# A hybrid layer step on one core: another order of loads and mixer work, and six constant matmuls ahead of the norm

## The reference

```python
xn = rms_norm(h, norm_mix); q, k, v, u = split(xn @ w_in, [512, 640, 768])
# attention: 8 heads of 64, 2 kv heads, window 128, ALiBi, sinks; samples attend a cache of 128
attn = window_attend(q, k, v, sinks)
# S5: 32 groups of 16 inputs and 64 complex states
lam_bar = exp(lam * step); b_bar = (lam_bar - 1) / lam * b
x[t] = lam_bar * x[t-1] + b_bar @ u[t];  y = gelu(real(c @ x) + d * u)
ssm = y * sigmoid(y @ w_glu + b_glu)
h = h + concat(rms_norm(attn), rms_norm(ssm)) @ w_out
h = h + moe(rms_norm(h))          # 32 experts, 4 per token, 1024 -> 2048 -> 1024, clipped SwiGLU
h = h + sigmoid(rms_norm(h) @ w_ple_gate) * (p @ w_ple_proj)
return rms_norm(h), new k and v windows, new states
```

## Time and profile before

| what | us |
|---|---|
| median of 3 runs (lowest, highest) | 1359.23 (1357.03, 1359.85) |
| the profiled execution | 1358.6 |
| its span | 1356.8 |
| TensorE busy in the span | 1239.3 (91%) |
| VectorE, ScalarE busy | 327.5 (24%), 200.7 (15%) |
| mean granted clock | 0.946 |
| first matmul of the output projection | 190.30 |

### The profile page before, as it was taken

One profiled execution on the slowest core, in us unless ns is written; L12 is line 12 of the kernel. 1 busy time (PEld: TensorE's weight loads), 2 busy tenths in 40 slices (PEclk: granted clock), 3 DMA queues, 4 the chain that ended last, 5 costly groups with the idle time before them and its releaser, 6 DMA issues.

```text
span 1356.8 us, 15894 instructions
## 1 busy us (share of the span) xinstructions
PE 1239.3 (91%) x6158; PEld 608.7 (45%) x6158; DVE 327.5 (24%) x574; ACT 200.7 (15%) x385; POOL 19.8 (1%) x51
## 2 busy tenths in 40 slices
PE   2689778989999999999999999999999999999875
PEld 2577556524344343434344443434344443434354
DVE  4862323202112211111212211111112211120132
ACT  3412521201010101101010101011011101110022
POOL 1000000000000000000000000000000000000000
PEclk9769679989999999999999999999999999998888
DMA  8004523297999999999999999999999999998500
GB/s 261 1 32 169 224 75 124 77 397 323 422 399 422 405 418 417 406 424 406 422 394 422 407 408 418 384 424 403 423 410 422 389 421 398 409 381 369 192 2 32
DMA packets 73262, 438.47 MB, mean 323 GB/s; under 512 B 13617, under 2 KB 16817, under 8 KB 22497
## 3 DMA queue, kind: packets, MB, share of 16 engines
q1 hardware_dynamic: 67264, 436.98, 79.1%
q10 hardware_dynamic: 5968, 1.08, 0.5%
HBM read 436.67 MB, written 2.41 MB: 324 GB/s over the span
## 4 chain that ended last, share of the span: by engine, by line
PE 87%; DVE 5%; ACT 4%; issue 2%; ACTq 2%; DVEq 0%
PE ps L895 38%; PE ps L912 18%; PE ps L881 10%; PE ps L851 5%; PE ps L784 2%; PE ps L1024 2%; PE ps L903 2%; PE ps L854 1%; PE ps L585 1%; ACTq L1052 1%; PE ps L967 1%; PE ps L921 1%; PE ps L720 1%; PE ps L567 1%; PE ps L661 1%
## 5 line engine op out<-in xcount | busy, mean ns | idle before, releaser
L895 PE MATMUL ps<-ring_up,region 128*64 128x512 f32 x2112 | 463.5, 596 | 2.6 <-issue 1.4
L895 PEld LDWEIGHTS ps<-ring_up,region 128*64 128x64 f32 x2112 | 164.2, 138 | 283.9 <-issue 282.1
L912 PE MATMUL ps<-ring_dn,region 128*64 128x512 f32 x1056 | 247.3, 623 | 12.4 <-issue 11.0
L1801 DVE TENSOR_SCALAR region<-ps 128x512 f32<-128x512 f32 x33 | 22.8, 692 | 716.4 <-PE ps L895 716.4
L912 PEld LDWEIGHTS ps<-ring_dn,region 128*64 128x64 f32 x1056 | 82.9, 143 | 163.5 <-issue 161.6
L881 PE MATMUL ps<-region,n_tok 128*128 128x128 f32 (+1 forms) x768 | 136.1, 307 | 0.0
L881 PEld LDWEIGHTS ps<-region,n_tok 128*128 128x128 f32 (+1 forms) x768 | 104.2, 187 | 41.2 <-issue 12.2
L1284 ACT ACTIVATE region<-region 128x512 f32<-128x512 f32 x33 | 20.8, 629 | 501.3 <-DVE region L1801 501.3
L1296 ACT ACTIVATE region<-ps 64x512 f32<-64x512 f32 x66 | 39.1, 592 | 270.3 <-PE ps L912 269.9
L851 PE MATMUL ps<-region 128*128 128x512 f32 (+1 forms) x136 | 65.9, 606 | 2.6 <-issue 1.3
L895 PE MATMUL ps<-region 128*64 128x512 f32 x264 | 62.7, 592 | 0.0
(11 more groups left out here) (361 smaller groups left out, 758.1 us busy)
## 6 DMA issues: line engine op xcount, KB each, us to landing
ring_up<-in_w_up_dram SPq DMA_DIRECT2D x264, 1024.0 KB, 11.9
ring_dn<-in_w_down_dram SPq DMA_DIRECT2D x132, 1024.0 KB, 7.7
ring_dn<-in_w_out_dram SPq DMA_DIRECT2D x1, 4096.0 KB, 21.2
ring_up<-in_w_ple_gate_dram SPq DMA_DIRECT2D x4, 1024.0 KB, 7.4
ring_up<-in_w_in_dram SPq DMA_DIRECT2D x2, 1536.0 KB, 16.8
ring_up<-in_w_in_dram SPq DMA_DIRECT2D x2, 1024.0 KB, 9.8
x_tok<-in_x_prompt_dram SPq DMA_DIRECT2D x2, 512.0 KB
ring_up<-in_w_glu_dram SPq DMA_DIRECT2D x1, 1024.0 KB, 5.6
```

The costliest lines, as they stand in the source:

```text
L895: m = mm(ps[64 * (q % 2):64 * (q % 2) + 64, q // 2, :], xe[:, k, slots] if k < UP else one_hot, w, start=(k == 0), stop=(k == UP))
L912: m = mm(ps[64 * half:64 * half + 64, O_B, :], act_t[:, f % 4, 64 * (f // 4):64 * (f // 4) + 64], ring_dn[:, f, 512 * half:512 * half + 51 ...
L1801: V.tensor_scalar(g_lim, bank(0), LIMIT, None, ALU.min).then_inc(Z["g_rdy"], 1)
```

## The change

In the diff "..." marks what is left out. The six small loads of b, c and the sample states leave ScalarE's queue and stand in SyncE's between the u columns and the q, k, v columns of w_in. The constants get a semaphore of their own, and TensorE multiplies six times the identity by the first 512 columns of the constants into bank 6, which nobody reads, when they are there. On all engines the mixer is reordered: the turning of c and of the states goes between u projections, the projections of k, v and q go between the pieces of the drive, the second half of the read-out matrix goes between the two scans, and in the second part the gated unit goes ahead of the samples' attention and the probabilities of block 1. The turnings of c and of the states, written in line before, become the functions `turn_outputs` and `turn_sample_states`. On ScalarE all copies of u come in one run ahead of the sines and of the copies of turned drive blocks. Banks change with it (`project_one`, `ssm_sums`).

```diff
--- before.py
+++ after.py
@@ -311,7 +312,7 @@
         @block.sync
         def _(sp):
             x_p, x_s = A["x_prompt"][0], A["x_sample"].rearrange("b l d -> (b l) d")
-            sp.dma_start(kst[:], A["shape_constants"]).then_inc(ld_x, 16)
@@ -323,9 +324,18 @@
-                    sp.dma_start(w_in[:, k:k + 4, cols], w[:, k:k + 4, cols]).then_inc(arrived, 16)
+            of_s5, of_heads = slice(D_IN - D_SSM, D_IN), slice(0, D_IN - D_SSM)
+            for k in range(0, KD, 4):
+                sp.dma_start(w_in[:, k:k + 4, of_s5], w[:, k:k + 4, of_s5]).then_inc(ld_wu, 16)
+            for r, name in enumerate(("ssm_b_re", "ssm_b_im")):
+                sp.dma_start(b_raw[:, r], A[name][0].rearrange("(k g) p h -> (g p) k h", g=2)).then_inc(ld_b, 16)
+            for r, name in enumerate(("ssm_c_re", "ssm_c_im")):
+                sp.dma_start(c_raw[:, r], A[name][0].rearrange("(k g) h p -> (g h) k p", k=4)).then_inc(ld_c, 16)
+            for r, name in enumerate(("state_ssm_re", "state_ssm_im")):
+                sp.dma_start(rows[:, (10 + r) * P:(11 + r) * P],
+                              A[name][0].rearrange("b (k g) p -> (b k) (g p)", g=2)).then_inc(ld_x0, 16)
+            for k in range(0, KD, 4):
+                sp.dma_start(w_in[:, k:k + 4, of_heads], w[:, k:k + 4, of_heads]).then_inc(ld_win, 16)
             sp.dma_start(sink_b, A["sinks"][0].partition_broadcast(P)).then_inc(ld_sink, 16)
             for b_ in range(NB):
                 sp.dma_start(sink_s[HEADS * b_:HEADS * (b_ + 1), :], A["sinks"][0].unsqueeze(1)).then_inc(ld_sink, 16)
...
@@ -452,7 +462,11 @@
         def _(pe):
             mm, tr = nc.tensor.matmul, nc.tensor.transpose
 
-            pe.wait_ge(ld_x, 64)
+            pe.wait_ge(ld_k, 16)
+            for _ in range(6):
+                mm(bank(6), ident, kst[:, 0:512], start=True, stop=True)
+
+            pe.wait_ge(ld_x, 48)
             pe.wait_ge(ld_vec, 16 * 7)
             tr(bank(7, V_N), rows[0:V_N, 0:P], ident[0:V_N, 0:V_N]).then_inc(Z["vec_ps"], 1)
 
...
@@ -588,11 +606,13 @@
 
             def project_one(n_):
 
-                slot, b = (4, 5, 0, 1, 2, 3)[n_], 6 + n_ % 2
+                slot, b = (4, 5, 0, 1, 2, 3)[n_], (6, 7, 2, 3, 2, 3)[n_]
                 if n_ == 0:
                     pe.wait_ge(ld_win, 32)
-                    pe.wait_ge(Z["x_states"], 1)
-                if n_ >= 2:
+                    pe.wait_ge(Z["turned_sb"], 2)
+                elif n_ == 2:
+                    pe.wait_ge(Z["us_sb"], 1)
+                elif n_ >= 4:
                     pe.wait_ge(Z["q_sb"], n_ - 1)
                 if slot >= 4:
                     m = project(slot, b, lambda k: w_in[:, k, D_ATTN + (slot - 4) * P:D_ATTN + (slot - 3) * P])
...
                     pe.wait_ge(Z["ssm_sq"], c + 1)
-                    m = mm(bank(5, T), ones, sq[:, c % 2], start=(c == 0), stop=(c == KM - 1))
+                    m = mm(bank(3, T), ones, sq[:, c % 2], start=(c == 0), stop=(c == KM - 1))
                     m.then_inc(Z["ssm_ssq"], 1)
 
             project_u(0)
             turn_parameters()
-            for j in range(1, 4):
-                project_u(j)
-            turn_drive()
+            project_u(1)
+            turn_outputs()
+            turn_sample_states()
+            project_u(2)
+            project_u(3)
+            project_one(0)
+            project_one(1)
+            turn_drive(range(4))
             drive(0)
+            project_one(2)
+            turn_drive(range(4, 8))
             drive(1)
+            project_one(3)
             drive_samples()
+            project_one(4)
             within_blocks()
-            for n_ in range(6):
-                project_one(n_)
+            project_one(5)
             kv_to_tokens()
             read_out_samples()
             scores(0)
             read_out(0)
             read_out(1)
             turn_states()
+            p_transposes(0)
             cache_transposes(0)
-            p_transposes(0)
+            values(0)
             cache_transposes(1)
-            values(0)
             scores(1)
+            gated_unit()
             sample_scores()
-            gated_unit()
+            ssm_sums()
             p_transposes(1)
             turn_sample_probs()
...
@@ -1044,14 +1071,6 @@
             act.dma_start(rows[0:ST, 14 * P:14 * P + 2], A["ssm_log_step"][0].rearrange("(k g) -> k g", g=2)
                           ).then_inc(ld_par, 16)
 
-            for r, name in enumerate(("ssm_c_re", "ssm_c_im")):
-                act.dma_start(c_raw[:, r], A[name][0].rearrange("(k g) h p -> (g h) k p", k=4)).then_inc(ld_c, 16)
-            for r, name in enumerate(("ssm_b_re", "ssm_b_im")):
-                act.dma_start(b_raw[:, r], A[name][0].rearrange("(k g) p h -> (g p) k h", g=2)).then_inc(ld_b, 16)
-            for r, name in enumerate(("state_ssm_re", "state_ssm_im")):
-                act.dma_start(rows[:, (10 + r) * P:(11 + r) * P],
-                              A[name][0].rearrange("b (k g) p -> (b k) (g p)", g=2)).then_inc(ld_x0, 16)
-
             def root(n_, c):
 
                 nt = CHUNKS[c][1]
...
                 if c == 0:
-                    act.wait_ge(ld_x, 64)
+                    act.wait_ge(ld_k, 16)
                     f(stat[:, 0, 3:4], eps, ACT.Sqrt)
+                    act.wait_ge(ld_x, 48)
                 f(n_tok[0:nt, c], x_tok[0:nt, c], ACT.Square, accum_out=stat[0:nt, c, 0:1]).then_inc(Z["norm_ssq"], 1)
                 root(0, c)
...
+            act.wait_ge(Z["par_ps"], 1)
+            f(pcols, ps[:, 6, 2 * P:2 * P + 6 * ST].rearrange("p (a b) -> p a b", a=6), ACT.Copy).then_inc(Z["par_sb"], 1)
...
+            act.wait_ge(Z["s5_sb"], 2)
+            act.wait_ge(Z["zeroed"], 5)
+            for r in range(2):
+                for par in range(2):
+                    g = slice(par * S, par * S + S)
+                    m = f(e_bd[r][g, :, 0, par], b_bar[g, r], ACT.Copy)
+            m.then_inc(Z["e_bd_sb"], 1)
...
-            act.wait_ge(Z["par_ps"], 1)
-            f(pcols, ps[:, 6, 2 * P:2 * P + 6 * ST].rearrange("p (a b) -> p a b", a=6), ACT.Copy).then_inc(Z["par_sb"], 1)
...
+            for q in range(4):
+                f(u_s[0:32, q::4], ps[32 * q:32 * q + 32, 0:4, SEQ:T], ACT.Copy)
+            f(proj[:, 6:10, SEQ:T], ps[:, 0:4, SEQ:T], ACT.Copy).then_inc(Z["us_sb"], 1)
+            qkv((0,))
             act.wait_ge(Z["phase"], 2)
             f(sin_t, cos_t, ACT.Sin, scale=6.283185)
             f(cos_t, cos_t, ACT.Sin, scale=0.5 * 6.283185).then_inc(Z["sines"], 1)
...
+            qkv((1,))
+            drive_copies(range(4))
+            qkv((2,))
+            drive_copies(range(4, 8))
+            qkv((3, 4))
...
                 f(k_sb, ps[:, 5].rearrange("p (c n) -> p c n", c=4), ACT.Copy).then_inc(Z["k_rdy"], 1)
+                qkv((5,))
                 act.wait_ge(Z["k_rdy"], 2)
...
             p_copies(0)
+            cache_copy(0)
             unit_input()
+            cache_copy(1)
             state_copies()
-            cache_copies()
-            att_square(0)
-            exps(1)
-            sample_exp()
-            p_copies(1)
             for c in range(KM):
                 act.wait_ge(Z["glu_ps"], c + 1)
                 if c >= 2:
                     act.wait_ge(Z["ssm_y"], c - 1)
                 f(glu_s[:, c % 2], bank(c, T), ACT.Sigmoid, bias=vecs[:, V_GLU + c:V_GLU + c + 1]).then_inc(Z["glu_sig"], 1)
-            state_stores()
-            att_square(1)
             for c in range(KM):
                 act.wait_ge(Z["ssm_y"], c + 1)
                 if c >= 2:
                     act.wait_ge(Z["ssm_ssq"], c - 1)
                 f(sq[:, c % 2], fb[:, 4 + c, :], ACT.Square).then_inc(Z["ssm_sq"], 1)
-
+            att_square(0)
+            exps(1)
+            sample_exp()
+            state_stores()
+            p_copies(1)
...
               ).then_inc(Z["s_groot"], 1)
             act.wait_ge(Z["ssm_ssq"], KM)
...
-            for r, op in ((1, ALU.subtract), (0, ALU.add)):
+
+            def read_matrix(r, op):
+
                 V.tensor_tensor(f1, every_step(c_cc[:, r], STEPS), per_step(0, STEPS), ALU.mult)
                 chain(V.tensor_tensor(f2, every_step(c_cc[:, 1 - r], STEPS), per_step(1, STEPS), ALU.mult))
                 for par in range(2):
                     g = slice(par * S, par * S + S)
                     m = V.tensor_tensor(f_bd[r][g, :, 1:, par], f1[g], f2[g], op)
                 chain(m)
-            V.engine_nop().then_inc(Z["f_sb"], 1)
+                V.engine_nop().then_inc(Z["f_sb"], 1)
+
+            dve.wait_ge(Z["turned_sb"], 1)
+            read_matrix(1, ALU.subtract)
 
             dve.wait_ge(Z["sines"], 1)
             chain(V.tensor_tensor(cos_t, cos_t, cos_t, ALU.mult))
...
@@ -1653,36 +1676,37 @@
                 for t in range(2, STEPS):
                     for q in range(4):
```

(17 more changed lines are left out.)

113 lines of the change are left out of this document (48 added, 65 removed).

## The result

The changed kernel took 1336.21 us (median of 4 runs, 1333.9 to 1337.63), the kernel before 1359.54 beside it (4 runs, 1357.03 to 1361.09): a ratio of 0.9829 [0.9808, 0.9849], 23.3 us less. The forecast was 1323 with a range of 1311 to 1336. The direction was right and the size was not: 13 us of the forecast's 36 are missing, and the median lies 0.2 us above the range. The profiled execution took 1336.66 us with a span of 1334.9.

What follows compares the result with a forecast made beforehand. The prediction took the bound to be engine waits delaying the output projection's start at 190.30 us; 31.3 us up to the scores plus 4.4 behind them brought it 35.7 earlier, from 1359.23 to 1323, range 1311 to 1336.

Steps and rivals of the forecast that it cites:

- The front: Loads and first square: with six loads off ScalarE's queue, first square and first projection come 12.6 us earlier (10.9 to 12.7).
- Rival B: At the head: the front does not move, ScalarE's freedom is worth 4 to 5 us instead of 12.6; 1331, chance 0.12.
- The constants: At the head: six constant matmuls, 5.8 us, run free before the first scaled rows and bring 0 us.
- Rival E: At the head: constants leave the clock falling as before, already the base; if they hold it, 1321; no chance given.
- The drive at 49.5: First drive: starts at 49.5 us, 17.9 earlier, runs at the low clock after a hole, and gives v_ps at 56.5.
- Rival A: First drive: the clock stays up, the drive takes 3.6 us, 5.5 us less before the scores; 1317, chance 0.22.
- Scan and second half: From v_ps to the scores: scans, second drive and remaining projections let the scores start at 90.4 us, before 121.66.
- first term: Everything up to the scores: they start 31.3 us earlier than in the kernel before.
- The read-out ends at +12: Behind the scores: the read-out ends 12 us after the scores start.
- second term: From scores to output projection: 64.2 us instead of 68.6, a gain of 4.4 us (bounds 12.6 and 0.6).
- Rival C: Behind the scores: exponentials and probability transposes behind the gated unit repay its early start, 0 to 4 us worse; 1328, chance 0.13.
- Rival D: Before the output projection: TensorE never regains the high clock, doubled work costs 59 us against 35.7; 1382, chance 0.03.

Runs made afterwards that it cites:

- the kernel with the fillers ahead of the scores alone: The changed kernel plus three matmuls of constants into an unread bank, in TensorE's hole before the first scores; 1322.19 us, ratio 0.9735.

## Why the prediction came out as it did

1. *The front, 12.6 us.* Right: 12.86 at the first square, 12.85 at the first projection. b's second load took 11.7 us from issue to landing instead of 23.6. The q, k and v columns of w_in took 8.9 instead of 16.8, but the two don't compare: they are issued at 18.1 us now, behind the small parts, and before at some 7 us, right behind the columns of u. The columns of u, ahead of both, took 9.8 us before and 8.9 now. They were there by about 28 us, far ahead of need. Rival B is out. The Trainium skill (DMA: Bandwidth & Descriptors, section on issuing engines) says that a second issuer saves only the time to initiate a DMA, usually small against the DMA itself. Here that time was not small: ScalarE needed 13.5 us to issue two loads and could do nothing else meanwhile, and the loads alone were worth 10.3 us.
2. *The constants, 0.* Right, by leaving them out. Their price was 5.8 us in the sum and 7.79 in the trace, and was hidden either way. Rival E held, as the base.
3. *The drive at 49.5 with the clock falling in the hole before it, v_ps at 56.5.* Right in this execution: 49.85, 7.09 us at 0.50, 57.04. One support was misread: the "hole of some 3 us" ahead of the second values (165.6 to 168.6 us) held 16 transposes and two small ones, and TensorE stood only 0.7 us of it. Rival A is no other mechanism but another outcome of the same hole: of the eleven profiled executions with this order and no filler ahead of the drive, one had it. In that one 37.5 us go by from the first drive to the scores, against 42.4 in the kernel with the fillers ahead of the scores alone: 4.9 us, close to the 5.5 of rival A. Single times of one kernel lie up to 10 us apart.
4. *Scan and second half, scores at 90.4.* Nearly right: 91.99. The projections end at 86.7 instead of 85.4, of which 0.4 to 0.7 us at a time is TensorE standing with nothing to wait for that the profile shows. The first term is 29.7 us instead of 31.3.
5. *"The read-out ends at +12", and the whole second term of +4.4.* This is the step that failed: +22.5, and the second term is -8.6. My own numbers had TensorE done at 85.4 and the scores at 90.4, a hole of 5 us as long as the one ahead of the drive, where I had taken the fall. I did not ask the same question a second time. I had even read that a read-out at full clock stays there (rival A), and did not ask what one does that starts at the low clock. The bounds of this term (+56 to +68) counted the clock in the values and in the unit, never in the read-out, so the range ended too low as well. (At its other end, 1317 as the lowest of this mechanism does not follow from the bound of +56, which gives 1315.) Putting the clock back gave 63.2 against my 64.2; that this is so close is in part luck, since the 64.2 hold 2.0 us of stores that cost nothing. Putting a hole of that length into the kernel before cost 13.4 us, 4.4 of them the added wait itself. That is the cause, shown from both sides.
6. *The gated unit ahead.* Its times were right with the read-out at full clock, except that the unit took 8.96 us instead of 7.2, since the clock fell in the 2.46 us ahead of it (0.50 at 118 to 120 us). But "gain" was the wrong word. I compared with the kernel before, in which the unit stood behind work at the low clock; the comparison that tells is with the old order in the new kernel, and that is 7.4 us faster on the path at the low clock and 6.8 at the full one (6.1 and 3.0 in the medians), because the exponentials there run beside the unit. Rival C named this mechanism with up to 4 us against me, and it was there beside the other loss, hidden in the 64.2. The stores, 2.0 us in my sum, cost nothing: ScalarE issues them beside the exponentials (144.94 to 146.76 us).
7. *Rival D.* Not so: under dense projections the clock rose, 0.77 at 60 to 62 us. But one of the terms that it doubled, 11 us of read-out, is the loss that came.
